# Encoder layer on one core: first row tile in two halves, a reordered last attention sum, and a last product in three parts

## What is computed

```python
h = rmsnorm(x, norm1_g)
proj = h @ w_in                    # 512 q, 128 k, 128 v, 512 pooling columns
a = block_swept_gqa(rope(rmsnorm(q)), rope(rmsnorm(k)), v)   # 8 heads of 64, 2 kv heads
p = multiscale_pool(u, w_pool, pool_scale)
x = x + concat(a, p) @ w_out
h2 = rmsnorm(x, norm2_g)
x = x + square(relu(h2 @ w_up)) @ w_down                     # 4096 hidden columns
```

## Time and profile before

| | us |
|---|---|
| median of 3 runs | 1469.5 (1468.85 to 1471.01) |
| the profiled execution | 1468.74 |
| its span, first to last instruction | 1467.0 |
| PE busy / DVE busy / ACT busy / POOL busy | 1460.4 / 1049.4 / 731.3 / 406.0 |

### The profile page before, as it was taken

The page is one execution under the profiler, slowest core; times in us unless marked ns, Lnnn a source line. Parts: engine busy times, 40 slices in busy tenths (PEclk is TensorE's granted clock), DMA queues, the critical chain, the costliest instruction groups (busy, mean ns, idle before and its releaser), DMA issues.

```text
span 1467.0 us, 23235 instructions
## 1 busy us (share of the span) xinstructions
PE 1460.4 (100%) x7810; PEld 1305.2 (89%) x7810; DVE 1049.4 (72%) x1241; ACT 731.3 (50%) x1255; POOL 406.0 (28%) x372
## 2 busy tenths in 40 slices
PE   9999999999999999999999999999999999999999
PEld 8999988888888889999999999998888888888887
DVE  7766799999868885444544454549887888878875
ACT  6233398898846755454545454546332323333220
POOL 3467587667735510000000000001230220311300
PEclk9999999999999999999999999999999999999999
DMA  8644341111346748433343334347644344343434
GB/s 266 154 116 118 86 127 39 34 25 25 94 156 233 261 189 342 155 119 130 114 159 121 124 114 159 133 179 282 230 156 159 101 157 138 111 152 112 140 94 184
DMA packets 94443, 212.30 MB, mean 145 GB/s; under 512 B 12080, under 2 KB 31408, under 8 KB 94256
## 3 DMA queue, kind: packets, MB, share of 16 engines
q1 hardware_dynamic: 92192, 200.46, 41.3%
q10 hardware_dynamic: 2192, 11.08, 1.8%
HBM read 133.08 MB, written 71.62 MB: 140 GB/s over the span
## 4 chain that ended last, share of the span: by engine, by line
PE 99%; DMA 0%; ACT 0%; DVE 0%; POOL 0%; issue 0%; ACTq 0%; POOLq 0%
PE ps L959 25%; PE ps L960 25%; PE ps L961 24%; PE ps L1235 6%; PE ps L1116 5%; PE ps L1245 3%; PE ps L1095 3%; PE ps L1131 3%; PE ps L1097 3%; PE ps L1132 3%; DMA g1c<-in_g 0%; PE ps L984 0%; PE ps L1022 0%; PE ps L1023 0%; PE ps L1027 0%; PE ps L993 0%
## 5 line engine op out<-in xcount | busy, mean ns | idle before, releaser
L959 PE MATMUL ps<-h,wuhi 128*128 128x384 f32 (+1 forms) x904 | 301.3, 333 | 0.2 <-issue 0.2
L961 PE MATMUL ps<-h,wulo 128*128 128x384 f32 (+1 forms) x904 | 301.1, 333 | 0.0
L960 PE MATMUL ps<-h,wuhi 128*128 128x384 f32 (+1 forms) x904 | 301.1, 333 | 0.0
L959 PE MATMUL ps<-wdhi,hidhi 128*128 128x512 f32 x672 | 261.5, 389 | 0.1
L960 PE MATMUL ps<-wdlo,hidhi 128*128 128x512 f32 x672 | 261.4, 389 | 0.0
L961 PE MATMUL ps<-wdhi,hidlo 128*128 128x512 f32 x672 | 261.4, 389 | 0.0
L2351 DVE TENSOR_TENSOR yacc<-yacc,ps 128x1024 f32<-128x1024 f32 x167 | 203.3, 1217 | 76.6 <-PE ps L961 76.6
L1368 ACT ACTIVATE hidhi<-hin 128x1024 fp32r<-128x1024 f32 (+1 forms) x72 | 86.9, 1207 | 300.7 <-PE ps L961 291.6
L2265 DVE TENSOR_TENSOR u<-u,ps 128x384 f32<-128x384 f32 x96 | 53.1, 553 | 181.5 <-PE ps L961 181.5
L959 PEld LDWEIGHTS ps<-h,wuhi 128*128 128x128 f32 x904 | 169.7, 188 | 0.6 <-issue 0.4
L960 PEld LDWEIGHTS ps<-h,wuhi 128*128 128x128 f32 x904 | 169.7, 188 | 0.0
(11 more groups left out here) (236 smaller groups left out, 2809.3 us busy)
## 6 DMA issues: line engine op xcount, KB each, us to landing
hd<-hout SPq DMA_DIRECT2D x64, 384.0 KB, 3.2
hin<-hd SPq DMA_DIRECT2D x48, 512.0 KB, 3.6
hd<-hout SPq DMA_DIRECT2D x32, 576.0 KB, 2.8
hin<-hd SPq DMA_DIRECT2D x24, 768.0 KB, 4.4
wuraw<-in_w_up SPq DMA_DIRECT2D x17, 1024.0 KB, 6.0
wdraw<-in_w_down SPq DMA_DIRECT2D x8, 2048.0 KB, 9.6
h<-h2d ACTq DMA_DIRECT2D x7, 1536.0 KB, 10.8
x2in<-in_x SPq DMA_DIRECT2D x12, 512.0 KB, 3.4
```

The lines of the kernel that those rows point to most:

```text
L959: pe.matmul(out, w_hi, m_hi, start=start, stop=False, skip_group_check=resumed)
L960: pe.matmul(out, w_hi, m_lo, start=False, stop=False, skip_group_check=resumed)
L961: return pe.matmul(out, w_lo, m_hi, start=False, stop=stop, skip_group_check=resumed)
```

## The change

The row order of `w_in` becomes two halves of four chunks (row h*512 + p*4 + k), so that chunks 0 to 3 need only the first 512 columns of x. Tile 0 is loaded in two DMAs of 256 KB with weight chunks 0 and 1 between them; the last four transposes move behind `high(0)` and `cross(0)`; ScalarE and VectorE run `split_first(1)` ahead of the wait for `g1c`; `low(k)` is placed anew. `g1c` is loaded as two runs of 16 B per partition in place of one of 32 B. Tiles 2 to 11 come as eight DMAs each with pieces of 512 B, and VectorE transposes each in two instructions. The tile of zeros shrinks from 512 to 128 columns.

At the end of attention, the first output product goes to banks 4 and 5 and no longer waits for `wf_lo` 3; `wolo` is moved in three DMAs (two rows after `wf_lo` 2, one after 3, one after 4); POOL's last `add_out` waits for `wo_lo` 4. The last output product is made column half by column half, each with its own count of `out_done`, and the left residual stands ahead of `lo_h2`. The last down product is made of three parts in banks of their own (512, 256 and 256 columns), and the running sum that stood under it is added before the sixth accumulation.

```diff
-        zeros = at("zeros", X + 11264, [512], F32R)
+        zeros = at("zeros", X + 11264, [P], F32R)
+        LAST_PARTS = ((0, 6, 0, 512), (1, 7, 0, 256), (1, 0, 256, 512))
+        def out_bank(p):
+            return 2 * (p % 2) if p else 4
-        w_rows = w_in.rearrange("(p k) n -> k p n", k=KT)
+        w_rows = w_in.rearrange("(h p k) n -> h k p n", h=2, k=KT // 2)
...
                 for q in range(4):
-                    sp.dma_start(quarter_in(t % 2, q), quarter_of(t, q)).then_inc(x_in[t % 2], 16)
+                    for h in range(2):
+                        sp.dma_start(quarter_in(t % 2, q, h), quarter_of(t, q, h)).then_inc(x_in[t % 2], 16)
...
-            sp.dma_start(xin[:, 0], x[0:P]).then_inc(x_in[0], 16)
-            for k in range(5):
+            sp.dma_start(xin[:, 0, 0:512], x[0:P, 0:512]).then_inc(first_in, 16)
+            load_wi(0)
+            load_wi(1)
+            sp.dma_start(xin[:, 0, 512:D], x[0:P, 512:D]).then_inc(x_in[0], 16)
+            for k in range(2, 5):
                 load_wi(k)
...
+                    sp.wait_ge(wf_lo, 2)
+                    sp.dma_start(wolo[:, 0:2].bitcast(F32), wqlo[:, 0:2].bitcast(F32)).then_inc(wf_moved, 16)
                     sp.wait_ge(wf_lo, 3)
-                    sp.dma_start(wolo[:, 0:3].bitcast(F32), wqlo[:, 0:3].bitcast(F32)).then_inc(wf_moved, 16)
+                    sp.dma_start(wolo[:, 2:3].bitcast(F32), wqlo[:, 2:3].bitcast(F32)).then_inc(wf_moved, 16)
...
                 for k in range(KT):
+                    if k == 1:
+                        pe.wait_ge(x_in[0], 16)
+                        turn_first(2)
+                        low(0)
                     if k == 5:
+                        low(4)
                         pe.wait_ge(x_in[1], 16)
...
-                    if k:
-                        low(k - 1)
+                    if k == 1 or k in (3, 4) or k > 5:
+                        low(k if k == 1 else k - 1)
...
-                if p < 2:
-                    pe.wait_ge(wf_lo, p + 3)
-                else:
+                if p == 1:
+                    pe.wait_ge(wf_lo, 4)
+                elif p:
                     pe.wait_ge(x2_done, p - 1)
...
+                if (u, o) == (UNITS - 1, SLOTS - 1) and last:
+                    for q, bank, c0, c1 in LAST_PARTS:
+                        for k in range(2):
+                            mm = three(ps[:, bank, c0:c1], hidhi[i][:, k, q, j], hidlo[i][:, k, q, j],
+                                       wdhi[z][o][:, k, c0:c1], wdlo[z][o][:, k, c0:c1], k == 0, k == 1)
+                        mm.then_inc(down_done if c1 == 512 and q else down_half, 1)
+                    return
...
+            def project_last():
+
+                p, i = TT - 1, (TT - 1) % 2
+                pe.wait_ge(c_lo, TT)
+                pe.wait_ge(x2_done, p - 1)
+                for h in range(2):
+                    bank, cols = out_bank(p) + h, slice(h * 512, h * 512 + 512)
+                    for n, (c, w) in enumerate(((chi, wohi), (clo, wohi), (chi, wolo))):
+                        if (h, n) == (1, 1):
+                            transpose_x2(p - 1)
+                        for j, k in enumerate(SLOT_ROWS):
+                            mm = pe.matmul(ps[:, bank], c[i][:, k], w[:, j, cols], start=(n == 0 and j == 0),
+                                           stop=(n == 2 and j == KT - 1))
+                    mm.then_inc(out_done, 1)
...
-            act.dma_start(g1c[:], g1.rearrange("(p k) -> p k", k=KT)).then_inc(g1_in, 16)
+            act.dma_start(g1c[:].rearrange("p (h k) -> p h k", h=2), g1.rearrange("(h p k) -> p h k", h=2, k=KT // 2)).then_inc(g1_in, 16)
...
             split_first(0)
+            split_first(1)
             act.wait_ge(g1_in, 16)
             split_wi(0)
-            split_first(1)
             split_wi(1)
             split_first(2)
...
                 else:
+                    residual_left()
                     lo_h2(p - 1)
-                    lo_wu(0, 2)
-                    residual_last()
-                    for o in (3, 5, 6):
+                    residual_right()
+                    for o in (2, 3, 5, 6):
                         lo_wu(0, o)
                     scale_last()
...
+                    else:
+                        q = acc_quarter(u, *QUARTERS[SLOTS - 1])
+                        dve.tensor_tensor(q, q, down_banks(u, SLOTS - 1), ALU.add).then_inc(acc_half, 1)
                     accumulate(n, u, 5)
...
                 if n == OUTS - 1:
-                    pool.wait_ge(wo_hi, 4)
+                    pool.wait_ge(wo_lo, 4)
```

More of the change, by code:

```diff
@@ L944, in _ @@
                         for j, t in enumerate((a, b)):
[L945 to L946 removed]
                             sp.dma_start(y[t * P:(t + 1) * P, cols], yacc[:, u, half, j, cols]).then_inc(y_out, 16)
[L948 removed]
+            sp.wait_ge(y_out, 16 * (4 * (UNITS + 1) + 2))
         @block.tensor
@@ L975, in project_qkv, with turn_first @@
                 mm.then_inc(qkv_done, 1)
+            def turn_first(h):
+                k0, k1, out = first_part(h)
+                for k in range(k0, k1):
+                    mm = pe.transpose(out[:, k - k0], row_in(0, k), ident[:])
+                mm.then_inc(xT_done if h == 2 else xT_half, 1)
             def first_qkv():
@@ L1030, in first_block @@
             def first_block():
-                pe.wait_ge(x_in[0], 16)
-                for h in range(3):
-                    k0, k1, out = first_part(h)
-                    for k in range(k0, k1):
-                        mm = pe.transpose(out[:, k - k0], row_in(0, k), ident[:])
-                    mm.then_inc(xT_done if h == 2 else xT_half, 1)
+                turn_first(0)
+                turn_first(1)
                 first_qkv()
@@ L1195, in warm @@
                 for _ in range(n):
-                    pe.matmul(ps[:, 4], zeros[:, 0:P], zeros[:], start=True, stop=True)
+                    pe.matmul(ps[:, 4].rearrange("p (k c) -> p k c", c=P), zeros[:], zeros[:].unsqueeze(1).to_broadcast([P, 4, P]),
+                              start=True, stop=True)
             pe.wait_ge(mexp_set, 1)
             warm(6)
-            pe.wait_ge(ident_in, 16)
+            pe.wait_ge(first_in, 2 * 16)
             first_block()
@@ L1328, in down_product @@
                                    wdhi[z][o][:, k], wdlo[z][o][:, k], o in OPENS and k == 0, k == 1, o not in OPENS)
-                    if q == 0 and (u, o) == (UNITS - 1, SLOTS - 1) and last:
-                        mm.then_inc(down_half, 1)
                 mm.then_inc(down_done, 1)
@@ L1336, in down_chunk @@
                         down_product(n, z, u, o, last)
-            for p in range(TT):
+            def project_last():
[11 more added lines that the diff above has]
+                    mm.then_inc(out_done, 1)
+            for p in range(TT - 1):
                 project_out(p)
+            project_last()
             up_product(0, 0, 1, 0, 0)
@@ L1412, in _ @@
             split_wi(4)
+            split_wi(5)
             square_x(0)
-            for k in range(5, KT):
+            for k in range(6, KT):
                 split_wi(k)
```

78 lines of the change are left out of this document (44 added, 34 removed).

## The result

The changed kernel takes 1472.07 us by the median of 22 runs (1470.86 to 1473.23), the kernel before, run beside it, 1469.01 (22 runs): a ratio of 1.0018, 95% interval 1.0012 to 1.0024. That lies above the predicted range, which ended at 1471.3, and 2.7 above the predicted time. The profiled execution took 1471.6 us around a span of 1469.8, 2.86 and 2.8 more than that of before.

A forecast was written before the change was run, and what follows sets the result against it. TensorE, busy 1460.4 of 1467.0 us, was taken as the bound, so only its waits could be won. +0.95 - 0.72 - 0.2 - 0.1 = -0.07 gave 1468.7, or 1469.4 us on the median's scale; range 1467.9 to 1471.3.

The forecast's parts named there:

- paid off the path: Later tiles: eight DMAs per tile and VectorE's second transpose instruction cost nothing; SP's queue some 2 us later per tile, covered.
- The term +0.95: Start: gain landing 0.45 us later plus 0.5 from moved work gives +0.95 us, bounds +0.2 and +1.3.
- Rival (b): Start: TensorE's clock falls while waiting for the gain; 1.6 us lost if once (chance 0.12), 3.0 if twice (0.04).
- the gain was not later: Start: the forecast had `g1c` land at 6.1 us in place of 5.69, 0.45 later.
- one for one: Start: SP's and ScalarE's queues alternate single pieces, 0.12 us a pair, so the gain's cost follows its number of pieces.
- rival (a): Start: the gain's doubled pieces pass in one turn, so it lands no later; start +0.2, sum -0.8 us; chance 0.13.
- First output product: End of attention: two TensorE stalls removed, 0.43 and 0.29, together -0.72 us; bounds -0.4 and -0.75.
- GpSimd's last sum: End of attention: starts at 410.93 behind the splits, ends at 413.9 us, covered by other work, cost nothing.
- Last output product: VectorE's scaling starts at 540.0, not 540.52, shortening TensorE's wait: -0.2 us, bounds +0.1 and -0.5.
- Tail: Behind the last matmul: shorter last addition, partly offset by smaller store pieces: -0.1 us, bounds 0 and -0.28.
- rival (c): Last output product and tail: moved waits only change place, stores hold the tail; time 1469.8 us; chance 0.09.

The follow-up runs named there:

- before_8: The kernel before with eight smaller-piece transfers in place of four for each later row tile, nothing else: 1471.16 against 1469.75 us, ratio 1.0010.
- pool_waits: The changed kernel with GpSimd's second subtraction of wq held until VectorE's subtraction of wp is done: 1470.29 us against 1469.57 for the kernel before, ratio 1.0007.
- wq_later: The kernel before with GpSimd's pair of wq subtractions made to wait until ScalarE has rounded wp: 1470.53 against 1469.91 us, ratio 1.0004.
- last_output: The kernel before with only the last output product as changed: 1470.65 against 1469.91 us, ratio 1.0001.
- start_wait: The kernel before with the change's start part, and GpSimd's second wq subtraction held until VectorE's of wp is done: 1470.31 against 1469.61 us, ratio 1.0006.
- start_only: The kernel before with only the change's start part, including eight transfers for each later tile: 1472.08 against 1469.57 us, ratio 1.0020.
- square_first: The changed kernel with GpSimd's second wq subtraction behind VectorE's of wp, and ScalarE's square back ahead of the sixth chunk: 1470.10 against 1469.91 us, ratio 0.9999.
- no_start: The change without its start part (first tile as before), against the kernel before: 1468.89 against 1469.57 us, ratio 0.9995.
- last_parts: The kernel before with only the last down product in three parts: 1469.78 against 1469.61 us, ratio 1.0001.

## Why the prediction was wrong

**The step that failed** is the one that put the eight transfers per tile among what is "paid off the path" and costs nothing. I looked for cover where the transfers run, and that cover held: VectorE's two waits on `xin` grew from 6.7 to 8.4 us in all, and no matmul was later for it. But the eight transfers changed when a much later one landed: that of `o_part` at 386 us, some 260 us behind the issue of the last of them, came 0.7 us sooner after its own issue. With it changed how GpSimd stood to VectorE. Before, VectorE's subtraction met the end of GpSimd's first one; after, it met the beginning of the second, and TensorE waited 1.47 us. That eight transfers in place of four do it is shown (before_8), that the two engines' overlap is the price too (pool_waits, wq_later). My theory of the shifted start is not needed: last_output, shifted by 3.18, has the subtraction at 1.09. Why the landing depends on the earlier transfers, and whether on their number or on that of their pieces, was not found. No row of before gave the size; one could have asked which short instruction stands within 0.1 us of TensorE's need, and this one did (391.58 for 391.63).

**Start.** The term +0.95 lies between what the profile showed (1.78) and what the averages show (0.6); its reasons were not all right. The first profile of before is one of the best starts: eleven profiles with the old start lag it by 0.97 on average (that one counted as 0), seven with the new start by 1.59. So the change's own cost is about 0.6, and 0.7 by start_wait, whose interval still holds zero. It goes with TensorE's clock. Where the first tile's matmuls ran at the upper level throughout, the old start lags 0.41 (six profiles) and the new 1.32 (two); where a stretch ran at the lower, 1.64 (five) and 1.69 (five). Rival (b)'s slow matmuls thus came in the profile that I compared, but not by its path: the clock did not fall in the wait, it had not yet risen, as in five of the eleven profiles with the old start. A clock that had risen and fell again is in start_only and square_first alone, both with the new start; two of seven against none of eleven is too few to say that the change brings it on. Of my reasons, the gain was not later: the pieces of the two queues did not pass one for one, as the earlier trace rows had led me to take it (20 and 103 in the densest 0.2 us), and for the landing rival (a) was right. What is left is what was moved: the transposes and first chunks behind the wait, and the square behind the sixth chunk, which I did not price. It puts the last chunk 0.73 later on ScalarE, but no run shows by itself what of this reaches TensorE.

**First output product.** Right in mechanism and size: -0.78 to -0.80 for -0.72 in all ten profiles with this part, both stalls gone as described. GpSimd's last sum, priced at nothing, ended at 418.26 us, 1.4 later than forecast once the lag of 3.0 is taken off: 0.9 of this is its addition, 2.21 us for 1.29 while two subtractions of VectorE ran beside it, the rest a later start. TensorE did not wait for it.

**Last output product.** Right at the place (-0.23 for -0.2; scaling 3.05 behind, as forecast), but not priced was what comes behind it. The up steps lose 0.01 to 1.36 in the nine profiles with this part, 0.68 on average, and -0.02 to 0.12 in the others but before_8 (1.07). The four with this part but without the eight transfers lose 0.26 on average, about what the part gains; the five with both lose 1.01 (0.45 to 1.36). The eight transfers without the part lost 1.07 in one profile of three and nothing in two. The chain is shown by the rows (store, relu, copy, TensorE); what decides its length in one execution is not. It is not that whatever was gained ahead is given back: before_8 had gained nothing, and no_start kept its gain.

**Tail.** Nothing, for -0.1, and last_parts agrees: rival (c) had the stores hold it. The last store is issued 0.2 us sooner against the last product, but lands 2.3 us behind its issue in place of 2.0.

The sum by averages, with 1.0 for the up steps from the five profiles that have both parts, is 0.6 + 1.6 - 0.8 - 0.2 + 1.0 = 2.2 and stands inside the interval of the ratio, 1.8 to 3.5 us.

## What to carry to other kernels

A part that is free where it runs can still move the engines against each other far behind it; before calling it free, list the short instructions that end within a few tenths of a microsecond of TensorE's need, and which of them share something with another engine. Where VectorE and GpSimd both work on SBUF operands close to a critical product, put them in an order by a wait: 0.68 us with it, up to 2.76 without. And a lag table of the same instruction in two traces finds such places in one look, but a single profile of a start is one draw: here the same code differed by up to 3 us.

## What the runs showed of the hardware

TensorE's clock at the launch does not follow the program alone. With identical code up to the first product, two matmuls took 0.59 and 0.51 from 6.79 us on in the kernel before, and 0.98 and 0.84 from 6.74 us on, with 0.84 still at 12.58, in last_output. In the profiles with the old start no clock fell again in the first tile once it was up. In start_only the granted clock was at the upper level, went to the lower, and rose again within the first tile; the stretches, with PE's busy time first and the granted clock, PEclk, third from the last:

```profile
4.40:7.70 3.30, 1.67 (x10) 1.15 (x9) 1.77 (x3) 2.52 (x4) 0.00 (x0) 1.00 0.97 347
7.90:11.10 3.20, 3.20 (x12) 2.78 (x11) 2.80 (x4) 2.69 (x4) 0.00 (x0) 0.50 1.03 408
11.30:14.00 2.70, 2.70 (x17) 2.34 (x16) 1.91 (x3) 1.62 (x3) 0.00 (x0) 1.00 1.03 411
```

In that execution TensorE had waited 1.62 us before its first product; the clock held through that product and fell during the four transposes behind it. In the profiles of last_output and of the changed kernel the same column reads 1.00 from the beginning, while the durations say otherwise until 13.8 and 10.2 us, so durations are the safer reading. And a transfer's time from issue to landing, same bytes and same engines, was 2.2 or 3.0 us by how many transfers, with how many pieces, its queue had carried long before. Its pieces moved at the same distance from the issue in both, the last at 1.8 us; what differs is when the sixteen signals of its completion came: from 1.97 to 2.25 us in the changed kernel and from 1.99 to 2.99 in the kernel before.
